# Delta rule: group decays from one product each, products ahead of the projections' barrier, blocks gathered before their ones

## The chip, the cores and the metric

The kernel runs on one core of one Trainium2 chip. Its engines work beside each other and meet at semaphores: PE (TensorE, matmuls into PSUM banks), DVE (VectorE), ACT (ScalarE), POOL (GpSimd) and SP, which issues the DMAs. The metric is the device time of one execution in microseconds (us).

## The reference

One layer of a hybrid network on 256 tokens of width 1024: modulation, input projections, a gated delta rule (8 heads, both directions), a state-space scan, an output projection and 32 experts of which 4 serve a token. What this change touches is the delta rule's triangular solve, per head and chunk of 64 tokens:

```python
G = jnp.cumsum(g, axis=-1)                        # g: log decay of a token
rel = G[..., :, None] - G[..., None, :]
kb = k * beta[..., None]
strict = idx[:, None] > idx[None, :]
lmat = jnp.einsum('bhncd,bhnsd->bhncs', kb, k) * jnp.exp(jnp.where(strict, rel, -jnp.inf))
mmat = lmat + jnp.eye(CHUNK, dtype=lmat.dtype)
rhs = jnp.concatenate([v * beta[..., None], kb * jnp.exp(G)[..., None]], axis=-1)
sol = lax.linalg.triangular_solve(mmat, rhs, left_side=True, lower=True, unit_diagonal=True)
```

Context and latent tokens make 512 tokens, 8 chunks of 64. The later scan over chunks uses `sol`; the experts come last.

## The kernel before

Every engine has its program written out by hand, in order. An engine marks a step on its own semaphore (`L.mark`) and another waits for that mark (`wait_ge(*L.at(engine, step, ...))`). All instructions of an engine run in the order in which the code issues them. The program has stages. In `proj` PE multiplies the tokens by the weight columns (`fm`, 20 of them) and by the modulation weights (`ada_chunk`, 12 of them), ACT copies and applies silu, DVE convolves (five taps a block, lines 1675 and 1680) and makes rows (`row_out`). At its end every engine marks `end` and waits for the other four (`barrier`).

The `delta` stage follows. Tokens lie in four tiles `t` of 128 (two chunks each); with two directions `d` this makes eight groups `G = 2t + d`, each of 8 heads x 64 columns = 512 columns. Tiles 0 and 1 are block `b = 0` of the solve, tiles 2 and 3 block 1. A group goes through these steps:

- POOL, `start_decay(G)` (line 2281), writes the mask less the second cumulative decay into one of four places, `DT[:, G % 4]`. From group 4 on it waits until group G - 4 is coupled.
- PE, `spread_decays(G)` (line 703), makes the first cumulative decay in a bank, by 16 products of 64x64: for each head and half a column of decays, broadcast, times a triangle of ones. An fp32 product is two matmul records in the trace, each with a weight load.
- DVE, `decay(G)` (line 1729), adds the two; ACT, `decays(G)` (line 1334), exponentiates; PE, `gram(t)` (lines 720, 725), makes k times k; DVE, `couple(G)` (lines 1740, 1743), multiplies into the matrix `MT`.
- POOL, `unit_diagonal(G)` (line 2307), puts ones on the diagonal by two selects.

Then, per block: PE gathers the 16x16 diagonal blocks (`gather_blocks`, line 735), DVE inverts them by substitution (`substitute`, lines 1751 to 1794, which leaves `Ysym`), PE scatters them back (`scatter_blocks`, line 746), DVE spreads them under masks into `X0` and `XT0` (`spread_inverses`, line 1807), and PE and DVE go up the levels 16 and 32 (`level_p`, line 760, `level` on DVE, `level_x`, `last_product`, `last_level`; lines 772 to 804), until `solved` (821, 833) forms W and U. Block 0 and 1 alternate on PE: gather 0, scatter 0, P 0, gather 1, the rest of level 0, scatter 1, and so on.

After this come the scan over the chunks (lines 849 to 983), the output projection (1022, 1028), routing, and the experts: a loop of turns, each of one expert and up to 64 rows (1097 to 1164). SP streams the expert weights in pieces of 2 MB through a ring of six.

## Time and profile before

| | |
|---|---|
| device time, three runs | 1454.61 us median, 1451.48 to 1460.07 |
| the profiled execution | 1451.1 us, span 1449.3 us |
| PE busy | 1276.2 us (88%) |
| DVE, ACT, POOL busy | 476.6, 253.0, 112.6 us |
| chain that ended last | PE 45%, DMA 28%, issue 4%, DVE 2%, ACT 2%, POOL 1% |
| mean DMA rate | 317 GB/s |

A share of busy time is a mean over the stages. The chain of waits is followed back from the last instruction: at each step to what released it. "issue" is time in which an engine waited for nothing that the profile shows. In a timeline row the bracket says how long the engine was idle before, and who ended it. The profiled execution is one run, so sums over its rows are to be held against its own 1451.1 us.

### The profile page before, as it was taken

Reading aid. Unit: us, or ns where it says so; the run is one execution under the profiler, and the core shown is the slowest. Engines: PE = TensorE matmul, PEld = TensorE weight load, DVE = VectorE, ACT = ScalarE, POOL = GpSimd, SP = SyncE. Lnnn points to the kernel's source line nnn. Section 1 sums busy time; section 2 is a strip of 40 time slices with the busy share of each in tenths; the row PEclk is TensorE's granted clock in tenths of the full one; section 3 lists DMA queues with packets and bytes.
Section 4 is the critical chain, followed back from the end, with each engine's and each line's share of the span. In section 5 each row is a group of like instructions: output and inputs, shape, how many; then the busy total and the mean of one; then the engine's idle time right before and its main releaser. Section 6 shows DMA issues by size and latency. Waiting matters only on the chain.

```text
span 1449.3 us, 27301 instructions
## 1 busy us (share of the span) xinstructions
PE 1276.2 (88%) x11256; PEld 593.7 (41%) x11257; DVE 476.6 (33%) x1023; ACT 253.0 (17%) x491; POOL 112.6 (8%) x158
## 2 busy tenths in 40 slices
PE   6999999456898999989898889887998999999995
PEld 2555445356665434333333333332433433433432
DVE  1246345651785523222221222121322322322323
ACT  2321522113614111111111111100100100100101
POOL 0201410443411000000000000000000000000000
PEclk9999999655997999999999999999999999999998
DMA  9516273000057699999999999999999699969993
GB/s 361 239 35 226 73 269 124 2 26 12 7 211 282 284 427 428 428 429 427 427 427 428 428 428 428 428 427 427 426 427 427 261 428 427 428 284 412 428 427 151
DMA packets 47824, 458.88 MB, mean 317 GB/s; under 512 B 4369, under 2 KB 4753, under 8 KB 22673
## 3 DMA queue, kind: packets, MB, share of 16 engines
q1 hardware_dynamic: 47762, 457.96, 76.2%
q8 instruction: 50, 0.82, 0.2%
q14 instruction: 12, 0.10, 0.0%
HBM read 456.31 MB, written 1.05 MB: 316 GB/s over the span
## 4 chain that ended last, share of the span: by engine, by line
PE 45%; DMA 28%; issue 4%; DVE 2%; ACT 2%; POOL 1%; DVEq 0%; ACTq 0%; POOLq 0%
DMA arena<-in_w_up 28%; PE bank L1135 21%; PE bank L1164 8%; PE bank L1106 3%; PE bank L1097 2%; PE bank L1028 2%; ACT arena L1517 1%; PE bank L1128 1%; PE bank L760 1%; PE bank L1159 1%; PE bank L1081 0%; PE bank L872 0%; PE bank L833 0%; PE bank L778 0%; POOL arena L2307 0%
## 5 line engine op out<-in xcount | busy, mean ns | idle before, releaser
L1135 PE MATMUL bank<-arena 128*64 128x512 f32 x2176 | 481.8, 595 | 34.6 <-DMA arena<-in_w_up 19.3
L1135 PEld LDWEIGHTS bank<-arena 128*64 128x64 f32 x2176 | 155.3, 136 | 342.1 <-issue 265.7
L1164 PE MATMUL bank<-arena 128*64 128x512 f32 x1088 | 239.4, 592 | 0.0
L2175 DVE TENSOR_SCALAR arena<-bank 128x512 f32<-128x512 f32 x34 | 23.6, 693 | 389.8 <-PE bank L1135 389.8
L1164 PEld LDWEIGHTS bank<-arena 128*64 128x64 f32 x1088 | 79.0, 136 | 137.6 <-issue 135.2
L634 PE MATMUL bank<-arena 128*128 128x512 f32 (+1 forms) x320 | 122.4, 539 | 0.4 <-DMA arena<-in_wfm 0.4
L2156 DVE TENSOR_TENSOR arena<-arena,bank 128x512 f32<-128x512 f32 x140 | 86.6, 682 | 6.0 <-PE bank L1106 6.0
L634 PEld LDWEIGHTS bank<-arena 128*128 128x128 f32 x320 | 60.5, 192 | 60.5 <-issue 54.1
L1097 PEld LDWEIGHTS bank<-arena 128*128 128x128 bf16 x1680 | 60.3, 118 | 27.0 <-DVE arena L2179 25.8
L1106 PE MATMUL bank<-arena 64*128 64x512 f32 x280 | 69.6, 614 | 0.9 <-ACT arena L1519 0.9
L1097 PE MATMUL bank<-arena 128*128 128x64 bf16 x1680 | 64.1, 199 | 1.1 <-DVE arena L2097 1.1
L1519 ACT ACTIVATE arena<-bank 128x512 f32<-128x512 f32 x34 | 20.4, 599 | 253.2 <-PE bank L1164 253.2
L2177 DVE TENSOR_SCALAR arena<-bank 128x512 f32<-128x512 f32 x34 | 23.6, 693 | 112.4 <-PE bank L1135 112.4
L2101 DVE TENSOR_SCALAR arena<-arena 96x64 bf16<-96x64 f32 x35 | 8.8, 251 | 156.8 <-PE bank L1164 156.8
L1511 ACT ACTIVATE arena<-arena 128x512 f32<-128x512 f32 x34 | 21.5, 632 | 212.9 <-DVE arena L2175 212.8
L1680 DVE SCALAR_TENSOR_TENSOR arena<-arena 128x512 f32<-128x512 f32 (+1 forms) x80 | 55.2, 690 | 2.8
L1511 ACT ACT_TABLE_LOAD x16 | 20.5, 1283 | 192.6 <-DVE arena L2175 192.6
L1513 ACT ACTIVATE arena<-bank 128x512 f32<-128x512 f32 x34 | 20.4, 600 | 190.2 <-PE bank L1097 190.2
L1106 PEld LDWEIGHTS bank<-arena 64*128 64x128 f32 x280 | 24.1, 185 | 45.8 <-issue 45.0
L1159 PE MATMUL bank<-arena 96*64 96x512 bf16 x68 | 13.8, 401 | 27.1 <-ACT arena L1517 27.1
L2164 DVE TENSOR_SCALAR arena<-arena 128x128 f32<-128x128 f32 x68 | 20.6, 346 | 43.0 <-issue 27.1
L567 PE MATMUL bank<-arena 128*128 128x512 f32 x64 | 29.7, 620 | 2.2 <-ACT arena L1207 2.2
(336 smaller groups left out, 1101.0 us busy)
## 6 DMA issues: line engine op xcount, KB each, us to landing
arena<-in_w_gate SPq DMA_DIRECT2D x64, 2048.0 KB, 21.2
arena<-in_w_up SPq DMA_DIRECT2D x64, 2048.0 KB, 22.8
arena<-in_w_down SPq DMA_DIRECT2D x64, 2048.0 KB, 20.7
arena<-in_w_ada SPq DMA_DIRECT2D x12, 2048.0 KB, 9.2
arena<-in_wfm SPq DMA_DIRECT2D x20, 512.0 KB, 6.5
arena<-in_wz SPq DMA_DIRECT2D x2, 2048.0 KB, 19.8
arena<-in_w_out SPq DMA_DIRECT2D x2, 2048.0 KB, 8.8
arena<-in_x SPq DMA_DIRECT2D x2, 1024.0 KB, 9.9
```

The lines of the kernel that those rows point to most:

```text
L567: last = mm(ps[t], xmT[:, k, base:base + 128], ada[:, m, k, :], start=(k == 0), stop=(k == KT - 1))
L634: last = mm(dst, win[:, i % 3, k, :], cols_, start=(k == 0), stop=(k == KT - 1))
L1028: last = mm(ps[2 + 2 * t + c_], mixT[:, k, 128 * t:128 * t + 128], wout[:, k, 512 * c_:512 * c_ + 512], start=(k == 0), stop=(k == KT - 1))
L1097: last = mm(ps[2][:, SLOT * k:SLOT * k + SLOT], hparts[:, s_, t, 512 * (k // 4) + k % 4:512 * (k // 4) + 512:4], Sb[:, t, :], start=(n == ...
L1106: last = mm(ps[3 + 2 * t + c_], GT[r, t, :], ysb[r, :], start=True, stop=True)
L1135: last = mm(ps[m][64 * c_:64 * c_ + 64, :], xcT[:, k, :], ring[:, 2 * h_ + m, k % 4, 512 * c_:512 * c_ + 512], start=False, stop=(k == KT ...
L1159: mm(ps[2][64 * c_:64 * c_ + 64, :], selb[0:96, :], bias[0:96, 2, 512 * c_:512 * c_ + 512], start=True, stop=False)
L1164: last = mm(ps[2][64 * c_:64 * c_ + 64, :], hidT[:, k % 4, 64 * (k // 4):64 * (k // 4) + 64], ring[:, 4 + h_, k % 4, 512 * c_:512 * c_ + 5 ...
L1511: f(hid[:, 1], hid[:, 0], ACT.Sigmoid, scale=ALPHA).then_inc(*L.mark("sig"))
L1680: v.scalar_tensor_tensor(out=dst, in0=src, scalar=convw[:, wi, tap:tap + 1], in1=dst, op0=ALU.mult, op1=ALU.add).then_inc(*L.mark("conv", i))
L2156: v.tensor_tensor(acc[:, t, s_], acc[:, t, s_], ps[3 + 2 * t + c_][:, :], ALU.add).then_inc(*L.mark(*(("acc",) if L.turn is not None else ...
L2175: v.tensor_scalar(hid[:, 0], ps[0][:, :], LIMIT, None, ALU.min).then_inc(*L.mark("a"))
```

## The change

1. `spread_decays(G)` on PE is one product of 128x512 instead of 16 of 64x64: the matrix `same` (ones within a chunk) times `steps[:, G]`. POOL makes `steps` in eight products ahead of its `end` mark, triangle times decay, as soon as `ada_chunk(10)` has been read (they lie in that chunk's memory).
2. PE marks its `end` but no longer waits at the barrier. It waits instead for the few steps whose banks or tiles it uses. The other four engines keep the barrier.
3. The groups have eight decay places (`DTs`): four more lie in the memory of `kdS`. `start_decay` of groups 4 to 7 waits for nothing but POOL's own steps. The products go to banks 0, 1, 4, 5, 0, 1, 0, 1.
4. `gather_blocks(b)` waits for the coupling (`MT`) instead of the ones. POOL writes the ones of block b after the gather and after `Ysym` b, and `level_p(b)` waits for them.
5. `kdS` is written after the last coupling. DVE spreads the inverses of block 0 ahead of the couplings of groups 6 and 7. ACT issues one exponential of a single column at the start of `delta`.

```diff
-            barrier(pe, L, "proj")
...
             def spread_decays(G):
 
-                t, d = divmod(G, 2)
-                if G >= 2:
-                    pe.wait_ge(*L.at("dve", "rel", G - 2))
-                for head in range(H):
-                    for half in range(2):
-                        r = slice(64 * half, 64 * half + 64)
-                        last = mm(ps[G % 2][r, 64 * head:64 * head + 64],
-                                  gA[r, t, d * 8 + head:d * 8 + head + 1].broadcast_to([64, 64]),
-                                  tri[r, d, 64 * half:64 * half + 64], start=True, stop=True)
-                last.then_inc(*L.mark("Gb", G))
+                pe.wait_ge(*L.at("pool", "steps", G))
+                if G >= 4:
+                    pe.wait_ge(*L.at("dve", "rel", (0, 1, 4, 5)[G - 4]))
+                mm(ps[g_bank[G]], const("same"), steps[:, G].rearrange("p h c -> p (h c)"), start=True, stop=True).then_inc(*L.mark("Gb", G))
...
             def gather_blocks(b):
 
-                pe.wait_ge(*L.at("pool", "unit", 4 * b + 3))
+                pe.wait_ge(*L.at("dve", "MT", 4 * b + 3))
...
             def level_p(b):
 
                 pe.wait_ge(*L.at("dve", "X0", b))
+                pe.wait_ge(*L.at("pool", "unit", 4 * b + 3))
...
+            pe.wait_ge(*L.at("act", "pad", NFM - 1))
+            pe.wait_ge(*L.at("act", "turned", TURNED[-1]))
             for G in range(4):
                 spread_decays(G)
+            pe.wait_ge(*L.at("pool", "kT", NKQ - 1))
+            pe.wait_ge(*L.at("act", "mod", 11))
             gram(0)
             gram(1)
+            pe.wait_ge(*L.at("dve", "row", 11))
             gram(2)
...
+            f(ssq[:, 0:1], const("eps"), ACT.Exp).then_inc(*L.mark())
             for G in range(8):
                 decays(G)
...
             decay(7)
+            spread_inverses(0)
             couple(6)
             couple(7)
-            spread_inverses(0)
...
             def start_decay(G):
 
                 t, d = divmod(G, 2)
-                if G >= 4:
-                    pool.wait_ge(*L.at("dve", "MT", G - 4))
                 pool.wait_ge(*L.own())
...
+            pool.wait_ge(*L.at("pe", "ada", 10))
+            for G in range(8):
+                t, d = divmod(G, 2)
+                pool.wait_ge(*L.own())
+                g_.tensor_tensor(steps[:, G], tric[:, d].unsqueeze(1).broadcast_to([P, H, C]),
+                                 gA[:, t, 8 * d:8 * d + 8].unsqueeze(2).broadcast_to([P, H, C]), ALU.mult).then_inc(*L.mark("steps", G))
...
             def unit_diagonal(G):
...
-                pool.wait_ge(*L.at("dve", "MT", G))
+                pool.wait_ge(*L.at("pe", "gathered", G // 4))
...
+            for G in range(4, 8):
+                start_decay(G)
             pool.wait_ge(*L.own())
             g_.memset(area("Y8"), 0.0).then_inc(*L.mark())
...
+            pool.wait_ge(*L.at("pe", "Gb", 7))
+            pool.wait_ge(*L.own())
+            g_.memset(area("XTf"), 0.0).then_inc(*L.mark("XTf"))
+            pool.wait_ge(*L.at("dve", "Ysym", 0))
             for G in range(4):
                 unit_diagonal(G)
-                start_decay(G + 4)
-            pool.wait_ge(*L.own())
-            g_.memset(area("XTf"), 0.0).then_inc(*L.mark("XTf"))
-            unit_diagonal(4)
-            unit_diagonal(5)
-            pool.wait_ge(*L.at("dve", "Ysym", 0))
-            unit_diagonal(6)
-            unit_diagonal(7)
             for G in range(4):
                 keg(G)
+            pool.wait_ge(*L.at("dve", "MT", 7))
             for t in range(2):
                 last_decays(t)
             pool.wait_ge(*L.at("dve", "Ysym", 1))
+            for G in range(4, 8):
+                unit_diagonal(G)
             for t in range(2, NT):
                 last_decays(t)
```

On POOL, from the start of `delta`, the rows stood like this before (L2319 the memset of `Y8`, L2307 the ones, L2281 `start_decay`, L2324 the memset of `XTf`):

```order
L2319 MEMSET arena 128x4x8
L2307 AFFINE_SELECT arena<-arena 128x512 x2
L2281 TENSOR_TENSOR arena<-arena 128x512
L2307 AFFINE_SELECT arena<-arena 128x512 x2
L2281 TENSOR_TENSOR arena<-arena 128x512
L2307 AFFINE_SELECT arena<-arena 128x512 x2
L2281 TENSOR_TENSOR arena<-arena 128x512
L2307 AFFINE_SELECT arena<-arena 128x512 x2
L2281 TENSOR_TENSOR arena<-arena 128x512
L2324 MEMSET arena 128x2048
L2307 AFFINE_SELECT arena<-arena 128x512 x8
```

Now they stand like this (L2285 `start_decay`, L2295 the steps, L2334 the memset of `XTf`, L2317 the ones, L2307 `keg`, L2323 `last_decays`):

```order
L2285 TENSOR_TENSOR arena<-arena 128x512 x4
L2295 TENSOR_TENSOR arena<-arena 128x512 x8
L2285 TENSOR_TENSOR arena<-arena 128x512 x4
L2329 MEMSET arena 128x256
L2331 MEMSET arena 128x4x8
L2334 MEMSET arena 128x2048
L2317 AFFINE_SELECT arena<-arena 128x512 x8
L2307 TENSOR_TENSOR arena<-arena 128x512 x4
L2323 TENSOR_TENSOR arena<-arena 128x512 x4
L2317 AFFINE_SELECT arena<-arena 128x512 x8
```

The ones have moved behind everything that the gather needs, and those of block 1 behind four `keg` and four `last_decays`.

On PE, from the end of the projections, it was before (L703 `spread_decays`, L720 `gram`; a number behind `x` is that of products):

```order
L678 MATMUL bank<-arena 128x512 [waits dve_proj,act_proj]
L703 MATMUL bank<-arena 64x64 [waits pe_proj,pool_proj,sp_proj,dve_proj,act_proj]
L703 MATMUL bank<-arena 64x64 x31
L703 MATMUL bank<-arena 64x64 [waits dve_delta]
L703 MATMUL bank<-arena 64x64 x15
L703 MATMUL bank<-arena 64x64 [waits dve_delta]
L703 MATMUL bank<-arena 64x64 x15
L720 MATMUL bank<-arena 64x64 x34
```

and at the gather (L735), two more groups behind it, the scatter (L746) and P (L760):

```order
L735 MATMUL bank<-arena 32x16 [waits pool_delta]
L735 MATMUL bank<-arena 32x16 x127
...
L746 MATMUL bank<-arena 32x32 [waits dve_delta]
L746 MATMUL bank<-arena 32x32 x63
L760 MATMUL bank<-arena 32x32 [waits dve_delta]
L760 MATMUL bank<-arena 32x32 x127
```

The same two places now (L703 again `spread_decays`, L717 `gram`; L732 gather, L743 scatter, L758 P):

```order
L682 MATMUL bank<-arena 128x512 [waits dve_proj,act_proj]
L703 MATMUL bank<-arena 128x512 [waits pe_proj,pool_proj,act_proj]
L703 MATMUL bank<-arena 128x512 [waits pool_proj] x3
L717 MATMUL bank<-arena 64x64 [waits act_proj,pool_proj]
...
L732 MATMUL bank<-arena 32x16 [waits dve_delta]
L732 MATMUL bank<-arena 32x16 x127
...
L743 MATMUL bank<-arena 32x32 [waits dve_delta]
L743 MATMUL bank<-arena 32x32 x63
L758 MATMUL bank<-arena 32x32 [waits dve_delta,pool_delta]
L758 MATMUL bank<-arena 32x32 x127
```

The first decay product no longer waits for SP or DVE, the gather waits for DVE instead of POOL, and P waits for POOL as well as DVE.

## Rows read from the trace of the kernel before

**Rows 1.** The page, part 2: granted clock of PE in 40 slices, in tenths.

```profile
PEclk9999999655997999999999999999999999999998
```

**Rows 2.** Chain of waits, 243 to 300 us: start, duration (us), what.

```profile
256.16 0.67 POOL arena L2307
256.96 0.67 POOL arena L2307
...
257.77 1.06 POOL arena L2281
...
291.11 2.55 PE bank L760 x170
```

**Rows 3.** Timeline, 230 to 292 us: start, busy us, instructions [idle before, releaser].

```profile
230.80 1.92 PE L518 MATMUL bank<-arena 128*32 128x512 f32 x16
...
243.01 1.02 PE L678 MATMUL bank<-arena 128*128 128x512 f32 x2
...
243.63 0.42 DVE L1675 TENSOR_SCALAR arena<-arena 128x256 f32<-128x256 f32 x1 [2.97 <-ACT arena L1293]
...
247.62 6.54 PE L703 MATMUL bank<-arena 64*64 64x64 f32 x125 [3.59 <-DVEq L1718]
...
249.83 0.69 DVE L1729 TENSOR_TENSOR arena<-bank,arena 128x512 f32<-128x512 f32 x1 [2.37 <-PE bank L703]
250.62 1.28 ACT L1334 ACT_TABLE_LOAD   x1 [4.04 <-DVE arena L1729]
...
251.92 1.15 ACT L1334 ACTIVATE arena<-arena 128x512 f32<-128x512 f32 x2
...
255.24 2.75 DVE L1743 TENSOR_TENSOR arena<-bank,arena 128x256 f32<-128x256 f32 x8 [0.27 <-PE bank L720]
...
266.29 2.69 PE L735 MATMUL bank<-arena 32*32 32x16 f32 x170 [8.27 <-POOL arena L2307]
...
270.06 1.46 PE L735 MATMUL bank<-arena 32*32 32x16 f32 x86 [1.08 <-issue]
...
271.56 0.69 DVE L1751 COPY arena<-bank 128x512 f32<-128x512 f32 x1 [6.42 <-PE bank L735]
...
285.43 1.28 DVE L1729 TENSOR_TENSOR arena<-bank,arena 128x512 f32<-128x512 f32 x2
...
285.57 2.04 PE L746 MATMUL bank<-arena 32*32 32x32 f32 x128 [9.71 <-DVE arena L1794]
...
289.76 2.49 DVE L1807 TENSOR_TENSOR arena<-bank,arena 128x512 f32<-128x512 f32 x4
```

**Rows 4.** Timeline at 329 us; queue row (packets, MB, share) of 291 to 372.

```profile
329.26 1.93 PE L760 MATMUL bank<-arena 32*32 32x32 f32 x128 [2.57 <-issue]
...
q8 instruction: 22, 0.36, 2.0%
```

**Rows 5.** Timeline: convolution taps beside POOL and alone; products on POOL.

```profile
160.09 4.49 DVE L1680 SCALAR_TENSOR_TENSOR arena<-arena 128x512 f32<-128x512 f32 x4
...
177.72 3.12 DVE L1680 SCALAR_TENSOR_TENSOR arena<-arena 128x512 f32<-128x512 f32 x4
...
356.09 4.40 POOL L2352 TENSOR_TENSOR arena<-arena 128x512 f32<-128x512 f32 x4 [11.40 <-PE bank L789]
```

**Rows 6.** Second block's steps; L833 in two stretches (busy, records, clock, DMA).

```profile
303.38 0.69 DVE L1751 COPY arena<-bank 128x512 f32<-128x512 f32 x1 [5.68 <-PE bank L735]
...
325.93 0.23 PE L760 MATMUL bank<-arena 32*32 32x32 f32 x1
...
334.00:345.00 11.00, 5.75 (x128) 5.63 (x128) 0.62 0.02 4
360.00:372.00 12.00, 4.31 (x128) 4.04 (x128) 0.88 0.02 4
```

**Rows 7.** Chain of waits at 597 us; instruction queue from 480 to the end.

```profile
597.44 25.69 DMA arena<-in_w_up
...
q8 instruction: 5, 0.08, 0.0%
```

More of the change, by code:

```diff
@@ L165, in lay_out_sbuf @@
     free = CONSTS["qmask"][0]
-    free = put(free, ("Z21", 128), ("T1", 128), ("own", 96), ("mX", 64), ("mQ", 64), ("negc", 128))
+    free = put(free, ("Z21", 128), ("T1", 128), ("own", 96), ("mX", 64), ("mQ", 64), ("negc", 128), ("tric", 128))
     assert free <= CONSTS["qmask"][0] + 256 * LEVELS.index(16)
@@ L299, in layer_program @@
         sM = DT
+        tric = view(area("tric"), 2, C)
+        steps = view(area("ada", 0, 4096), 8, H, C)
+        g_bank = (0, 1, 4, 5, 0, 1, 0, 1)
+        DTs = [DT[:, G] for G in range(4)] + [view(area("kdS", 512 * G, 512), H, C) for G in range(4)]
         xw = [view(area("MT", 2048, 2048), 2, 2, H, C), view(area("keG"), 2, 2, H, C)]
@@ L1333, in decays @@
                 act.wait_ge(*L.at("dve", "rel", G))
-                f(DT[:, G % 4], DT[:, G % 4], ACT.Exp).then_inc(*L.mark("DT", G))
+                f(DTs[G], DTs[G], ACT.Exp).then_inc(*L.mark("DT", G))
             def inverses(b):
@@ L1728, in decay @@
                 dve.wait_ge(*L.at("pool", "NG", G))
-                v.tensor_tensor(DT[:, G % 4], view(ps[G % 2][:, :], H, C), DT[:, G % 4], ALU.add).then_inc(*L.mark("rel", G))
+                v.tensor_tensor(DTs[G], view(ps[g_bank[G]][:, :], H, C), DTs[G], ALU.add).then_inc(*L.mark("rel", G))
             def couple(G):
@@ L1737, in couple @@
                 for par in range(2):
-                    bk, DT_ = ps[(6 if t == 2 else 2) + par], DT[:, G % 4, par:8:2]
+                    bk, DT_ = ps[(6 if t == 2 else 2) + par], DTs[G][:, par:8:2]
                     if t >= 2:
@@ L2234, in _ @@
                 g_.tensor_copy(negc[r], neg[r, :, 64 * half:64 * half + 64]).then_inc(*L.mark())
+                pool.wait_ge(*L.own())
+                g_.tensor_copy(tric[r], tri[r, :, 64 * half:64 * half + 64]).then_inc(*L.mark())
             own = view(area("own"), 3, 32)
@@ L2277, in start_decay @@
                 t, d = divmod(G, 2)
-                if G >= 4:
-                    pool.wait_ge(*L.at("dve", "MT", G - 4))
                 pool.wait_ge(*L.own())
-                g_.tensor_tensor(DT[:, G % 4], negc[:, d].unsqueeze(1).broadcast_to([P, H, C]),
+                g_.tensor_tensor(DTs[G], negc[:, d].unsqueeze(1).broadcast_to([P, H, C]),
                                  Gs[:, t, 8 * d:8 * d + 8].unsqueeze(2).broadcast_to([P, H, C]), ALU.subtract).then_inc(*L.mark("NG", G))
@@ L2319, in _ @@
             g_.memset(view(area("Y8"), 4, 64)[:, :, 0:64:9], 1.0).then_inc(*L.mark("Y8"))
+            pool.wait_ge(*L.at("pe", "Gb", 7))
+            pool.wait_ge(*L.own())
+            g_.memset(area("XTf"), 0.0).then_inc(*L.mark("XTf"))
+            pool.wait_ge(*L.at("dve", "Ysym", 0))
             for G in range(4):
                 unit_diagonal(G)
-                start_decay(G + 4)
-            pool.wait_ge(*L.own())
-            g_.memset(area("XTf"), 0.0).then_inc(*L.mark("XTf"))
-            unit_diagonal(4)
-            unit_diagonal(5)
-            pool.wait_ge(*L.at("dve", "Ysym", 0))
-            unit_diagonal(6)
-            unit_diagonal(7)
             for G in range(4):
                 keg(G)
+            pool.wait_ge(*L.at("dve", "MT", 7))
             for t in range(2):
```

## The prediction

> **What bounds the kernel now.** I read the page first, then the chain of waits, then the waits of PE, then the timeline around the places that the diff touches. Behind the projections, which end at about 247 us, the page's row of the granted clock falls to 0.6 and 0.5 for three slices [rows 1]: there PE often waits, and this is where the diff works. The chain of waits goes PE, DVE, POOL, DVE, PE there [rows 2, 3]. The reader is to see four things in it.
>
> First, the projections' barrier: PE's last projection product starts at 243.01, but the decay products start at 247.62, released by DVE, 3.6 us later [rows 3]. Second, POOL: after the first couplings (DVE, 255.24 to 258.0) POOL writes ones on the diagonal by pairs of selects 0.80 us apart, with a decay start of 1.06 us between pairs, and only when the fourth pair ends does PE gather the diagonal blocks, at 266.29 [rows 2, 3]. PE waited 8.3 us for it, and 9.7 for DVE's substitution behind it [rows 3]; no other wait of PE between 244 and 372 is as long. Third, that substitution runs from the copy at 271.56 to 285.51, and the level's product P starts at 291.11, after DVE has spread the inverses from 289.76 [rows 2, 3]. Fourth, from 291 on the PE waits for nothing but "issue": 128 matmul records run in 1.9 us, then 1.3 to 2.6 us of nothing. In the same stretch the instruction queue moved 22 blocks, 0.36 MB, so 16 KB each, one per 3.7 us [rows 4]. I read this as PE waiting for its instructions. A stretch so bound shifts with its start; it does not shrink by faster engines.
>
> The Trainium skill, "Runtime: NRT & Kernel Launch", Instruction fetch mechanics, also says that instructions come in blocks of 16 KiB, but calls the crossing of a boundary mostly hidden. By that sentence a product removed here would be worth nothing anywhere and the stretch would be set by the matmuls; the gap of 2.57 us in [rows 4] contradicts it.
>
> **The change part by part.**
>
> *One product per group instead of 16.* A group's decay took 32 matmul records (256 for eight groups), and takes 2 now: 240 records less, 1.9 blocks of 128. At 3.7 us a block that is 7.0 us if the PE were fetch-bound there, and 0 if it waits for others there. Six of the groups stand before the gather, two before the scatter, ahead of waits of 8.3 and 9.7 us [rows 3]; I take 0. The new product is 128x512 in fp32; the row product of that size took 1.02 us [rows 3]. Four of them from 244.1 end near 248, and grams 0 to 2, 128 records, near 250 (128 took 1.93) [rows 4], when DVE has done its adds.
>
> *Steps on POOL.* Eight products of 128x512 at 1.10 us (four took 4.40) are 8.8 us [rows 5]. They may start when the tenth ada chunk has been read, at 232.7 [rows 3], and end at 241.6. POOL was idle up to the barrier; PE wants the first at 244.1. They run beside DVE's convolutions. There the trace has a price: four convolution taps took 4.49 us beside POOL and 3.12 alone [rows 5]. Two such blocks are met in part: at most 2 times 1.4 us, against 2.97 us in which DVE idles before the last convolution [rows 3]. I take 0; were that idle time missing it would cost 2.8.
>
> The Trainium skill, "SBUF — State Buffer", Who interferes with whom, has a rule that speaks against this part: a DVE instruction with two SBUF inputs contends with a GpSimd instruction that reads SBUF. The 4.49 against 3.12 agree with it. By the rule each engine may block the other whole; even with the whole 2.8 us on POOL the last step would end near 244.4.
>
> *No barrier for PE.* DVE, ACT and POOL keep it, so the adds still start at 247.6. What goes is that PE's products stood behind it: the first add started at 249.83 [rows 3], now at 247.6, 2.2 us earlier. The exponential's table load of 1.28 us, which followed the first add [rows 3], now runs beside it.
>
> *From the barrier to the gather.* DVE: four adds at 0.64 (two in 1.28) are 2.6, eight couplings 2.75 [rows 3]: 247.6 + 2.6 + 2.75 = 253.0. ACT's first exponential can run at 247.6 + 1.28 + some 0.2 = 249.1, and four at 0.58 (two in 1.15) end at 251.4, so it is not late. The gather waits for the fourth coupling and no longer for POOL: 253.1 instead of 266.29, **13.2 us** earlier. Queued behind it on PE are the last two decays and gram 3, which DVE wants only after the substitution. The gather keeps its 5.2 us (266.29 to 271.5, one fetch gap of 1.08 within) [rows 3]. The four extra decay places let POOL start groups 4 to 7 at once (four at 1.06 from 247.6), so the fifth add no longer waits for POOL: two adds and the next couplings, 1.3 and 2.8 us, end at 257.1, before the gather does at 258.3. If they were late, the substitution behind them on DVE would be late by as much; with 1.2 us of room I take 0.
>
> *Substitution.* 13.95 us as before, from the copy at 271.56 to 285.51, where the scatter is released [rows 3]. Ysym is ready at 272.3 instead.
>
> *Ones behind the substitution.* POOL now writes them when Ysym is there, and the level's product P waits for the fourth pair: eight selects at 0.80 and two hand-overs of 0.1 are 6.6 us [rows 2]. Before, P started 5.6 us after Ysym (291.11 less 285.51) [rows 2]. So **1.0 us is lost** here. This is the new wait. It also hides the edit that puts the spreading before the last couplings: X0 would be ready 3.4 us after Ysym (scatter 2.04, half of 2.49, a hand-over) [rows 3], and nobody is waiting for it alone. Priced alone, that edit is worth between 0 and 2.2; I take 0.
>
> *The rest of the delta rule.* P starts at 278.9, and the fetch-bound chain follows, **12.2 us** earlier as a whole. The place of the block edges moves by 16 records or so, which is some 0.5 us either way and at worst one gap, 1.9. The second block's ones could be late too: its substitution starts with a copy at 303.38 [rows 6], so it ends at 317.3, now 305.1; the ones end at 311.7, and its P, at 325.93 before [rows 6], is due at 313.7. They are 2.0 us early. What POOL does behind them comes 6.5 us later against the chain; before 356.09 POOL idled 11.4 us [rows 5].
>
> *Experts.* No DMA is added or moved in SP's queue, and its waits are for steps of PE in this chain; the first expert pieces wait for PE's transposes of the mixed rows. So the weight stream moves with the chain, and with it the DMA waits that bound later turns, the first at 597.44 [rows 7]. The 12.2 us pass whole to the end.
>
> **The sum.** -13.2 + 1.0 = -12.2 on a profiled execution of 1451.1 us (span 1449.3, 1.8 around it): 1438.9. The three runs had a median of 1454.6, 3.5 above the profiled one; with that offset the forecast is 1442. What this kernel's measurement can tell from no change is about 0.5%, 7.3 us.
>
> **The rivals.**
>
> *A, the ones cost twice.* If selects beside DVE stretch as the taps did (1.44 times), eight take 9.2 instead of 6.4: 2.8 late at the first P and, less the 2.0 of room, 0.8 at the second; a block edge in a bad place adds 1.9. Gain 12.2 - 5.5 = 6.7, so 1448. For it: POOL gets both sets of ones at the moment when DVE goes on. Against it: the selects stood 0.80 apart in [rows 2] while DVE worked on banks, which is what it will do again behind both substitutions. Chance 0.13.
>
> *B, more than forecast.* In 334 to 345 PE is bound by its own products, at a mean clock of 0.62: one line's 128 records took 5.75 us there and 4.31 in 360 to 372 at 0.88 [rows 6]. If the moved stretch meets the full level (2.4 GHz) more often, this line and its neighbour give back up to 3.5: gain 15.7, 1439. It may as well go against, by as much; I count that in the range. Chance 0.10.
>
> *C, slower.* The experts' loop must stay in PE's instruction store: from 480 us to the end only 5 blocks came on the instruction queue [rows 7], in 34 turns of a loop. The change moves the loop against the 16 KB edges. If a turn then had to fetch once more, at a gap of about 1.9 us, 33 turns would cost 63: 1442 + 63 = 1505. It decides as soon as more than 10 turns pay. Against it: the loop is no longer than before, and touches three blocks of 16 KB in either program. Chance 0.05.
>
> *Forecast*: 0.72.
>
> **How the numbers follow.** The predicted time is the forecast's, 1442. Its own range, 1438 to 1447, is the block edge, the clock, and the 3 us by which medians of three runs differ (before: 1451.5 to 1460.1). A and B lie at its edges, so 1435 to 1450 leaves out C and the tails. Faster by over 0.5%: most of the forecast (0.66), all of B (0.10), a third of A (0.04), 0.80. Within: 0.15. Slower: C, 0.05.
>
> **What would show it.** Right: the gather on PE starts near 253 and is released by DVE; the level's first product is released by POOL's select, near 279; the add of group 0 starts at 247.6 with no wait for PE; the gaps from 280 on are still "issue", 22 blocks or so; turns of experts as before. Wrong: the gather waits for ACT or for POOL's steps; the second P is released by POOL; instruction blocks fetched in most expert turns; DVE's adds later than 248.

## The result, and the profile after

The changed kernel runs in 1446.41 us (median of 8 runs, 1442.0 to 1451.61), the kernel before beside it in 1454.86 (8 runs, 1451.48 to 1460.07). The ratio is 0.9934, with a 95% interval of 0.9913 to 0.9955: 9.6 us faster, between 6.5 and 12.7. The forecast was 1442, range 1435 to 1450. Its gain of 12.2 us, a ratio of 0.9916, lies inside the interval; its time is 4.4 us below the median. The profiled execution took 1448.96 us, 10 more than the sum of the prediction.

| | before | after |
|---|---|---|
| span of the profiled execution | 1449.3 us | 1447.1 us |
| PE busy | 1276.2 us | 1279.4 us |
| POOL busy | 112.6 us | 123.0 us |
| instructions; instruction blocks on q8 | 27301; 50 | 26834; 48 |

The timeline of the changed kernel where [rows 3] stood, PE, DVE, ACT and POOL mixed (start, busy us, instruction; in brackets idle before and releaser):

```profile
234.07 10.08 POOL L2295 TENSOR_TENSOR arena<-arena 128x512 f32<-128x512 f32 x8 [46.86 <-PE bank L522]
...
238.51 4.72 DVE L1684 SCALAR_TENSOR_TENSOR arena<-arena 128x256 f32<-128x256 f32 x4
...
244.24 1.02 PE L682 MATMUL bank<-arena 128*128 128x512 f32 x2
...
244.86 0.42 DVE L1679 TENSOR_SCALAR arena<-arena 128x256 f32<-128x256 f32 x1 [0.17 <-ACT arena L1296]
245.31 2.05 DVE L1684 SCALAR_TENSOR_TENSOR arena<-arena 128x256 f32<-128x256 f32 x4
...
245.57 3.68 PE L703 MATMUL bank<-arena 128*128 128x512 f32 x8 [0.30 <-PEq L688]
...
249.12 2.49 DVE L1733 TENSOR_TENSOR arena<-bank,arena 128x512 f32<-128x512 f32 x4 [0.42 <-DVEq L1722]
251.52 2.74 DVE L1747 TENSOR_TENSOR arena<-bank,arena 128x256 f32<-128x256 f32 x8
...
254.31 3.38 PE L732 MATMUL bank<-arena 32*32 32x16 f32 x221 [1.07 <-DVE arena L1747]
...
259.87 0.69 DVE L1755 COPY arena<-bank 128x512 f32<-128x512 f32 x1 [1.50 <-PE bank L732]
...
273.78 1.47 POOL L2317 TENSOR_SCALAR_AFFINE_SELECT arena<-arena 128x512 f32<-128x512 f32 x2 [8.37 <-DVE arena L1798]
275.45 1.47 POOL L2317 TENSOR_SCALAR_AFFINE_SELECT arena<-arena 128x512 f32<-128x512 f32 x2 [0.20 <-POOL arena L2317]
...
278.79 1.47 POOL L2317 TENSOR_SCALAR_AFFINE_SELECT arena<-arena 128x512 f32<-128x512 f32 x2 [0.20 <-POOL arena L2317]
...
280.36 2.25 PE L758 MATMUL bank<-arena 32*32 32x32 f32 x152 [4.65 <-DVE arena L1747]
284.27 1.61 PE L758 MATMUL bank<-arena 32*32 32x32 f32 x104 [1.67 <-issue]
```

The order of events is the one forecast: products behind the projections without a pause, adds, couplings, gather, ones behind the substitution, P. The wait of 4.65 us before P is put down to a coupling, but the couplings that P waits for (groups 0 to 5) had ended at 258.4; what ended at 280.26 is POOL's last select. Both programs are best compared from the last row product of the projections (L678 of before, L682 of after), because its own time changes from execution to execution; "at 36.1" below means 36.1 us behind that product. Against it the gather starts at 10.07 us instead of 23.28 and P at 36.12 instead of 48.10: 13.2 and 12.0 us earlier, as the sum had it.

Then the gain shrinks in this execution. The first KV product (L943) starts 121.53 us behind the row product, before 129.60: 8.1 us are left. The read-out behind the scan (L967) starts at 154.93 against 156.16: 1.2 left. The router's product (L1084) stands at 209.48 against 212.30: 2.8 left. So 3.9 of the 12.0 us went between P and KV, and 6.8 in the scan, before 1.6 came back. Where the scan's part went stands in the chain of waits of after (start, us, what):

```profile
390.06 1.06 PE bank L921 x32
391.12 2.00 PE bank L870 x4
393.12 1.06 PE bank L943 x32
394.18 2.00 PE bank L870 x4
```

In the kernel before the same four products took this:

```profile
388.88 1.09 PE bank L872 x4
```

And the windows of after (us, busy and count of PE, PEld, DVE, ACT, POOL, granted clock, DMA share, GB/s):

```profile
366.00:382.00 16.00, 12.38 (x377) 9.98 (x368) 10.41 (x24) 13.35 (x47) 8.93 (x9) 0.86 0.01 3
382.00:400.00 18.00, 18.00 (x216) 12.39 (x220) 8.80 (x19) 3.73 (x16) 10.09 (x10) 0.50 0.26 90
```

The scan ran at the lower of the two clock levels (1.2 GHz) here, and PE, which elsewhere waits in it, became its bound.

### The profile page after: what moved, and what is told of

Same layout as the page of the kernel before. It is cut to its first block, busy times and chain, and to the rows that moved or that the text cites. A ratio compares the mean times of both kernels' runs of the same rounds, so it can differ in the third digit from the quotient of the medians.

```text
span 1447.1 us, 26834 instructions
## 1 busy us (share of the span) xinstructions
PE 1279.4 (88%) x11016; PEld 586.6 (41%) x11017; DVE 479.3 (33%) x1023; ACT 253.1 (17%) x492; POOL 123.0 (8%) x168
## 4 chain that ended last, share of the span: by engine, by line
PE 41%; DMA 28%; DVE 2%; ACT 1%; issue 1%; DVEq 0%; ACTq 0%
DMA arena<-in_w_up 28%; PE bank L1138 21%; PE bank L1167 8%; PE bank L1109 3%; PE bank L1100 2%; PE bank L1031 2%; PE bank L870 1%; ACT arena L1521 1%; PE bank L1131 1%; PE bank L1162 1%; ACT arena L1519 0%; PE bank L974 0%; PE bank L986 0%; PE bank L996 0%; PE bank L1042 0%
## 5 line engine op out<-in xcount | busy, mean ns | idle before, releaser
L2181 DVE TENSOR_SCALAR arena<-bank 128x512 f32<-128x512 f32 x34 | 23.6, 693 | 112.6 <-PE bank L1138 112.6
L1684 DVE SCALAR_TENSOR_TENSOR arena<-arena 128x512 f32<-128x512 f32 (+1 forms) x80 | 58.7, 733 | 2.8
```

The source lines that it names most:

```text
L1684: v.scalar_tensor_tensor(out=dst, in0=src, scalar=convw[:, wi, tap:tap + 1], in1=dst, op0=ALU.mult, op1=ALU.add).then_inc(*L.mark("conv", i))
```

## The experiments

Theory 1: the change brings some 12 us, and what the trace lost behind P is drawn anew in each execution (the clock's level, the arrival of instruction blocks). Rival: a part of the loss is built in.

**The same kernel again.**

> The changed kernel once more, for a second trace. In its first trace the gather came 13.2 us earlier after PE's last row product (10.1 us after it instead of 23.3), but only 1.6 us were left at the first expert turn: 4 us went in the stretch where PE waits for instructions, 8 us in the scan over the chunks, where the granted clock was 0.5 and the two input products of a step took 2.07 us instead of 1.13. Theory 'level': the scan's clock differs from execution to execution; this trace may have it at 1.0, and then the last transposes of the mixed rows come about 8 us earlier than in the first trace; over the runs the ratio stays between 0.990 and 0.996. Rival 'built in': the moved stretch always meets the scan at 0.5; the second trace has 2.07 us again, and the scan takes 8 us more than before in every trace.

Measured: 1445.55 us, ratio 0.9932 [0.9906, 0.9959], span 1441.8. The scan of this execution:

```profile
366.00:382.00 16.00, 11.95 (x380) 9.75 (x380) 11.52 (x27) 12.69 (x45) 9.27 (x9) 1.00 0.01 3
382.00:400.00 18.00, 15.69 (x446) 12.58 (x444) 13.56 (x27) 4.39 (x19) 12.05 (x12) 1.00 0.43 142
```

Same program, full level (2.4 GHz), and its chain runs mostly through POOL and DVE where PE stood in the other. The read-out starts at 145.28 and the router's product at 201.71: 10.6 us before the old kernel's. From KV to the read-out it took 25.0 us, the first execution 33.4: the level cost 8.4. The fourteen profiles of this document agree: the stretch from KV to read-out took 25.0 us in the five whose granted clock over it was 1.00, 26.4 to 27.0 in the seven at 0.94, 27.6 in the one at 0.89, and 33.4 in this first one at 0.68. In the window before, where the clock of the first execution already fell to 0.86, PE was busy for 12.38 us of 16 in one and 11.95 in the other: why the clock fell in one and not in the other stays open. The two also differ by 1.25 us at KV.

**PE's barrier back.**

```diff
             pe.nop().then_inc(*L.mark("end", "proj"))
+            barrier(pe, L, "proj")
```

> The changed kernel with PE's barrier put back. My theory: the first product ends 0.9 us after 3.5 us of delay, so DVE's first add starts 0.9 to 1.0 us later after the barrier and the fourth ends 1.5 us later, since a product takes 0.86 us and an add 0.64; the gather starts 1 to 1.5 us later after PE's last row product (11.1 to 11.6 us instead of 10.1). Rival: the couplings wait for ACT's exponentials anyway, and the gather moves by under 0.5 us.

Measured: 1452.08 us, ratio 0.9969 [0.9951, 0.9988]. The gather starts at 13.94 us, 3.9 later than without the barrier and more than either expectation had (11.1 to 11.6, or under 0.5 later). The timeline of this kernel:

```profile
248.82 5.37 PE L704 MATMUL bank<-arena 128*128 128x512 f32 x8 [3.59 <-DVEq L1723]
...
250.43 0.69 DVE L1734 TENSOR_TENSOR arena<-bank,arena 128x512 f32<-128x512 f32 x1 [1.77 <-PE bank L704]
```

Its window from 249 to 256, which holds its eight decay records, and the window of the repeated changed kernel that holds the same eight, from 247:

```profile
249.00:256.00 7.00, 7.00 (x134) 3.70 (x135) 3.42 (x6) 3.81 (x6) 4.62 (x6) 0.76 0.00 0
```

```profile
247.00:254.00 7.00, 6.70 (x139) 3.93 (x139) 6.40 (x13) 3.68 (x7) 2.96 (x3) 1.00 0.02 5
```

The barrier costs twice: the adds start later by 1.3 us (6.2 behind the row product instead of 4.9), and behind the wait of 3.6 us the clock was granted at 0.76, so that eight records took 5.37 us instead of 3.68. The second and third add came 1.4 to 1.5 us behind the one before, and the fourth started 3.3 us later than without the barrier. The 1.7 us that the eight records took longer are what the clock added; by that estimate the barrier at full clock would cost the other 2.2. The lower clock is no accident of one execution: from 4.6 to 11.6 us behind the row product it was granted at 0.58 to 0.76 in all four profiles in which PE waits at the barrier (both of before, part 4 alone, this one), and at 1.00 in all ten in which it does not. The time is 6.5 us above that of the repeated changed kernel, timed beside it, where P is only 3.5 to 3.8 later; the difference is within the intervals and no run explains it.

**Sixteen products per group again**, over the broadcast decay as before; POOL's steps are still made and waited for.

```diff
-                mm(ps[g_bank[G]], const("same"), steps[:, G].rearrange("p h c -> p (h c)"), start=True, stop=True).then_inc(*L.mark("Gb", G))
+                t, d = divmod(G, 2)
+                for head in range(H):
+                    for half in range(2):
+                        r = slice(64 * half, 64 * half + 64)
+                        last = mm(ps[g_bank[G]][r, 64 * head:64 * head + 64],
+                                  gA[r, t, d * 8 + head:d * 8 + head + 1].broadcast_to([64, 64]),
+                                  tri[r, d, 64 * half:64 * half + 64], start=True, stop=True)
+                last.then_inc(*L.mark("Gb", G))
```

> The changed kernel, but a group's decay is again 16 products of 64x64; POOL still makes its steps, which nobody uses. The prediction priced the single product at 0, as work ahead of a wait: then the gather starts within 0.5 us of 10.1 us after the last row product, and P and the second gather too. Rival: the 240 more matmul records cost up to 1.9 instruction blocks of 3.7 us, 7 us, since the stretch before the gather is no longer covered by a wait for POOL; then the gather ends 2 to 4 us later.

Measured: 1447.33 us, ratio 0.9949 [0.9921, 0.9977]. The gather starts at 10.06, unchanged: the records ahead of it cost nothing, as the prediction took. Behind it they cost a little: DVE's copy starts at 16.22 instead of 15.62 and 15.34, and P at 36.70, 0.6 to 0.9 later, the router's product at 204.14. There are 50 instruction blocks instead of 48. That the two blocks cost time later is possible (1.8 us between the medians), but the intervals overlap: open.

**Before, with part 4 of the change alone**: the gather waits for the coupling, the ones stand behind the substitution, P waits for them.

```diff
-                pe.wait_ge(*L.at("pool", "unit", 4 * b + 3))
+                pe.wait_ge(*L.at("dve", "MT", 4 * b + 3))
...
                 pe.wait_ge(*L.at("dve", "X0", b))
+                pe.wait_ge(*L.at("pool", "unit", 4 * b + 3))
...
-                pool.wait_ge(*L.at("dve", "MT", G))
+                pool.wait_ge(*L.at("pe", "gathered", G // 4))
...
```

> The kernel before with one part of the change alone: the blocks are gathered after the coupling, ones are written behind the substitution, P waits for them; four decay places, 16 products, PE at the barrier. Theory: DVE's fourth coupling ended at 258.0, so the gather starts near 258.1 instead of 266.3 on the clock of the first trace, 8.2 us earlier after the last row product (15.1 us instead of 23.3), and P starts 7 us earlier. The other parts are then worth 5 us of the 12. Rival: the four decay places alone hold the couplings of groups 4 and 5, the substitution is late by several us and less than 5 us is left at P.

Measured: 1450.85 us, ratio 0.9967 [0.9946, 0.9988]. The gather stands at 14.55, 8.7 us earlier than before. About 8.3 of them are the wait for POOL's ones; the other 0.4 is that the fourth coupling itself ended 0.4 earlier, in an execution whose clock behind the barrier was 0.76 and not 0.58. P stands at 41.29, 6.8 earlier (expected: 7), and KV at 123.68. Of the 13.2 us at the gather the barrier is 3.9, and the remaining 0.6 (14.55 against the 13.94 of the kernel with the barrier) is the single product and the places.

**Ones beside the substitution.**

```diff
-            pool.wait_ge(*L.at("dve", "Ysym", 0))
             for G in range(4):
                 unit_diagonal(G)
```

> The changed kernel, but POOL writes the first block's ones as soon as the blocks are gathered, beside DVE's substitution, not behind it. In the changed kernel's two traces the level's first product P starts 36.1 and 35.8 us after the projections' last row product, 6.7 us after Ysym. Theory 1 (the ones behind the substitution are the 1.1 us that the change loses): POOL's selects run while DVE works through chains of small instructions whose time is mostly their fixed cost, the substitution keeps its 14.0 us, P waits for the spread alone and starts 3.4 to 4 us after Ysym, about 33 us after the row product, and the kernel is 2.5 to 3 us faster than the changed one (ratio to the kernel before 0.991). Rival (contention): selects and substitution stretch each other as taps and POOL did (4.49 against 3.12); the 6.6 us of selects lengthen the substitution by 2 us or more, P starts at 35 or later, and the kernel is within 1 us of the changed one.

Measured: 1443.24 us, ratio 0.9902 [0.9865, 0.9939]. P is at 34.96, 0.9 to 1.2 us earlier: both mechanisms happened. POOL and DVE in this kernel:

```profile
274.60 2.79 POOL L2317 TENSOR_SCALAR_AFFINE_SELECT arena<-arena 128x512 f32<-128x512 f32 x2 [0.20 <-POOL arena L2317]
```

```profile
270.22 2.85 DVE L1780 TENSOR_TENSOR arena<-arena 128x512 f32<-128x512 f32 x2
273.10 1.22 DVE L1783 TENSOR_REDUCE arena<-arena 128x128 f32<-128x1024 f32 x1
274.36 2.51 DVE L1786 TENSOR_TENSOR arena<-arena 128x512 f32<-128x512 f32 x2
...
279.29 1.21 DVE L1798 COPY arena<-arena 128x64 f32<-128x64 f32 x2
```

The same lines without selects beside them, in the changed kernel:

```profile
265.80 2.06 DVE L1780 TENSOR_TENSOR arena<-arena 128x512 f32<-128x512 f32 x2
267.89 1.22 DVE L1783 TENSOR_REDUCE arena<-arena 128x128 f32<-128x1024 f32 x1
269.14 2.05 DVE L1786 TENSOR_TENSOR arena<-arena 128x512 f32<-128x512 f32 x2
...
273.28 0.34 DVE L1798 COPY arena<-arena 128x64 f32<-128x64 f32 x2
```

A pair of selects grew from 1.47 to as much as 2.79 us, the two groups of products by 0.8 and 0.5. P stands 3.45 us behind the scatter instead of 6.7, but the scatter comes 2.1 to 2.3 later (21.4 us behind the gather instead of 19.1 to 19.4). Not all of this is the selects: `keg`, which follows them on POOL, started early too, at 279.27, and beside it the two copies that end the substitution (L1798) took 1.21 us instead of 0.34. The reduction, which reads one input, kept its 1.22. By the Trainium skill, "SBUF — State Buffer", Who interferes with whom, a DVE instruction with two SBUF inputs contends with a GpSimd one that reads, and a reduction never does; the rows of the products and of the reduction agree.

**Ones waited for piece by piece.** POOL writes the pairs in P's order.

```diff
-                pe.wait_ge(*L.at("pool", "unit", 4 * b + 3))
...
                     for u in range(16):
+                        if u % 8 == 0:
+                            pe.wait_ge(*L.at("pool", "unit", 4 * b + u // 4 + d))
...
-            for G in range(4):
+            for G in (0, 2, 1, 3):
                 unit_diagonal(G)
...
-            for G in range(4, 8):
+            for G in (4, 6, 5, 7):
                 unit_diagonal(G)
...
```

> The changed kernel, but P waits for the ones piece by piece: the first quarter of its products for the first pair of selects, and so on, and POOL writes the pairs in the order of P. Theory 1: P starts when the spread is there, 3.4 to 4 us after Ysym (about 33 us after the last row product instead of 36), and its last quarter no earlier than the fourth pair, 6.7 us after Ysym; it ends 1.5 to 2.5 us earlier than now, the instruction block that it needs is fetched meanwhile, and the kernel is 1.5 to 2.5 us faster than the changed one. Rival: behind P the PE waits for instructions, one block per 3.8 us, and the gap that P now runs over falls elsewhere; gain 0 to 0.5.

Measured: 1441.45 us, ratio 0.9891 [0.9847, 0.9935]; P at 32.76, 3.1 to 3.4 us earlier. The selects keep their 1.47 us, and P now waits for the spread:

```profile
277.14 2.25 PE L759 MATMUL bank<-arena 32*32 32x32 f32 x152 [1.41 <-DVE arena L1812]
280.71 1.61 PE L759 MATMUL bank<-arena 32*32 32x32 f32 x104 [1.32 <-issue]
```

At the second P (67.25 against 71.03 and 72.60) and at KV (116.27 against 120.28 and 121.53) it is still there, which speaks against the rival. But the kernel with two edits undone, below, with the same PE code as the changed one and P at 35.9 and 36.1, has KV at 117.57 and 119.97, so a lucky execution of the changed kernel comes within 1.3 us of this one; over the four such profiles the mean is 119.8, 3.6 later. At the router's product only 0.6 is left in this profile (201.15 against 201.71): its scan took 26.4 us and the better of the other two 25.0, and from read-out to router it took 58.4 against 56.4.

**One instruction block more**: 64 products of the second gather issued twice.

```diff
+                    if b and c_ < 16:
+                        for i in range(4):
+                            r = quarter(i)
+                            own = slice(32 * i + 16 * (c_ // 16), 32 * i + 16 * (c_ // 16) + 16)
+                            last = mm(ps[(4, 0)[b]][r, 16 * c_:16 * c_ + 16], MT[r, b, :, 32 * (i % 2) + c_], ident[r, own],
+                                      start=True, stop=True)
                 last.then_inc(*L.mark("gathered", b))
```

> The changed kernel with 64 more products (128 matmul records, one instruction block of 16 KB) in the second gather, which write the same values once more. Theory (PE is bound by its instructions from P to KV): from the gather on all is 3.7 to 4.0 us later against the last row product, though the 128 records themselves run in 1.9 us; KV starts at 124 to 125.5 instead of 120.3 and 121.5, and the instruction queue moves 49 blocks instead of 48. Rival (the gaps are waits for other engines' data, which the profile does not name): the records fill gaps, and KV is later by 0 to 1.9 us.

Measured in one execution: 49 blocks. The product behind that gather (XQ) stands at 52.44, against 48.21 and 49.55: 2.9 to 4.2 us later, more than the 1.9 us in which 128 records run. At KV only 0.9 is left against one profile of the changed kernel and nothing against the other (121.15; 120.28, 121.53). So the block costs its interval where it stands, but the spread of the arrivals behind it is as large. At KV the theory's 124 to 125.5 did not come, and what came (nothing to 0.9) is in the rival's range. That PE is bound by its instructions is supported at the one place, not shown for the stretch.

**Two edits undone**: places shared, and spreading behind the last couplings.

```diff
-        DTs = [DT[:, G] for G in range(4)] + [view(area("kdS", 512 * G, 512), H, C) for G in range(4)]
+        DTs = [DT[:, G % 4] for G in range(8)]
...
-            spread_inverses(0)
             couple(6)
             couple(7)
+            spread_inverses(0)
...
             for G in range(4, 8):
+                pool.wait_ge(*L.at("dve", "MT", G - 4))
                 start_decay(G)
...
```

> The changed kernel with two of its edits undone: groups 4 to 7 of the decays share the places of 0 to 3 again (POOL starts each behind its coupling), and the spreading stands behind the last couplings again. The prediction took both at 0. If that holds: gather at 10.1 us after the last row product as in the changed kernel, the substitution starts at 15.6 to 16.0, P at 35.8 to 36.2, released by POOL's ones. If the places matter, the adds of groups 4 and 5 wait for POOL and the substitution's copy starts later than 16.5; if the spreading matters, P is released by DVE, at 36.5 to 39, since decays 6 and 7 (1.3), couplings 6 and 7 (2.8) and the spread (3.4) add up to 7.5 us behind Ysym against the ones' 6.7.

Measured in one execution: gather at 10.07, the copy at 15.63, P at 36.11. POOL's last select ended at 36.0, so P was still released by the ones. At P both edits are worth nothing, as taken. But this execution needed 81.5 us from P to KV, and the changed kernel 84.4 and 85.4, which asked for another run:

> The kernel with the two edits undone (shared places, spreading behind the last couplings) once more, now timed. Its one profile had 81.5 us from the first P to the first KV, where the changed kernel had 84.4 and 85.4. Theory 1 (drawn anew in each execution): this profile has 82 to 85 us, and the ratio to the kernel before is that of the changed kernel, 0.993, within 0.002. Rival (the two edits cost what the trace of the changed kernel lost): 81 to 82 us again, and a ratio of 0.991 or less.

Measured: 84.1 us this time, and 1444.09 us, ratio 0.9927 [0.9902, 0.9952]. The same program drew 81.5 and 84.1. In both profiles the second P stands at 68.92 and 69.93, 1.1 to 3.7 us ahead of the changed kernel's, where DVE still has to couple groups 6 and 7 between the spreading and the first level; whether the edit costs something there, two profiles of each and the times do not tell.

**The kernel before once more.**

> The kernel before once more, for one profile. Theory 1 (how long PE takes from the first P to the first KV is drawn anew in each execution, since each of the 22 instruction blocks arrives after 3.4 to 4.0 us): the stretch takes 82 to 85 us, where the profile before had 81.5 and the profiles of the changed kernel 84.4 and 85.4; the last row product starts anywhere from 243 to 250, with the granted clock of the first 72 us. Rival (built in: the change put the block edges in worse places, and the stretch of the kernel before is short): again 81.0 to 82.0. In both, gather at 23.3 and P at 48.1 after the last row product, within 0.3.

Measured: 1454.54 us, gather at 23.17, P at 47.97, P to KV 82.6 us (81.5 in the first profile), router's product at 215.91 (212.30). The kernel before has now 81.5 and 82.6, kernels with the changed PE code 81.5 to 85.4 in four profiles, with means of 82.0 and 83.9. The two ranges overlap, but a built-in loss of some 2 us is not excluded. The first profile of before had drawn well at the start and from P to the router's product.

The start is the largest draw. The last row product, behind identical work, started at 243.01 in before and at 250.34 in the kernel with part 4 alone. Their first 36 us:

```profile
0.00:36.00 36.00, 23.57 (x115) 7.99 (x116) 5.33 (x21) 7.97 (x13) 0.20 (x4) 0.95 0.96 361
```

```profile
0.00:36.00 36.00, 20.98 (x87) 8.14 (x89) 5.32 (x21) 7.38 (x12) 0.20 (x4) 0.82 0.96 361
```

**Pieces, and x loaded later.**

```diff
-            sp.wait_ge(*L.at("pe", "scattered", 1))
+            sp.wait_ge(*L.at("pe", "W", 3))
             load("x", xin, x.rearrange("(t p) d -> p t d", p=P))
...
```

> The changed kernel with P waiting for its ones piece by piece, and with the load of x issued behind the last W product instead of behind the second scatter. In nine profiles the interval between instruction blocks that holds this load was 4.7 to 5.1 us, against a mean of 3.7 to 3.85. Theory 1 (load and instruction fetch share the DMA engines): no interval above 4.4 us remains between P and KV, the stretch is 1.0 to 1.5 us shorter than the 83.5 of the kernel with the pieces alone, and the ratio to the kernel before is 0.987 to 0.990. Rival: that interval is long for another reason (an instruction block that two engines want), and stays; ratio 0.989 to 0.992. Either way KV starts at 114.5 to 117 after the last row product (120.3 and 121.5 in the changed kernel).

Measured: 1441.28 us, ratio 0.99 [0.9869, 0.9932]. The x load was issued at 313.73 in the changed kernel; the gap of PE behind it:

```profile
320.72 1.93 PE L758 MATMUL bank<-arena 32*32 32x32 f32 x128 [3.34 <-issue]
```

In this kernel, at the same place (line 759), with the load at 359.47:

```profile
317.76 1.93 PE L759 MATMUL bank<-arena 32*32 32x32 f32 x128 [1.70 <-issue]
```

The long gap went: the block interval there is 3.5 us, where the twelve profiles with the load at its old place have 4.7 to 5.1. The interval that holds the later load is 5.3 us, but the kernel with the pieces alone has 5.5 there without a load. One of 4.6 us stands near 352 in this kernel with no load beside it, so "none above 4.4" was missed, and the load is not the only cause of a long interval. P to KV still took 83.4 us, and KV stands at 116.27 in both kernels: the load does slow a block, and moving it bought nothing that can be told.

**The second recurrence's decays as single products too**, over four steps that POOL writes into the place of x, whose load waits for them.

```diff
-                        last = mm(bk[r, 64 * head:64 * head + 64], gA[r, 2 + t, ch:ch + 1].broadcast_to([64, 64]),
-                                  tri[r, d, 64 * half:64 * half + 64], start=True, stop=True)
...
+                pe.wait_ge(*L.at("pool", "ssteps", G))
+                mm(bk, const("same"), ssteps[:, G].rearrange("p h c -> p (h c)"), start=True, stop=True).then_inc(*L.mark("sG", G))
...
```

> As the kernel before it in this list, and the four decays of the second recurrence (64 products, 128 matmul records) become one product each over steps that POOL makes, as the change did for the first eight; x is loaded once the fourth of them has been read. Theory 1 (PE is bound by its instruction blocks here, so 60 records fewer before KV are worth half a block, and 60 in the scan some of the other half): KV starts 1 to 2 us earlier than in the other kernel, the ratio to the kernel before is 0.985 to 0.988. Rival (POOL: 4.4 us more in front of its last keG groups, which W waits for): W2 is released by POOL and later by 1 to 2 us, ratio 0.989 or more.

Measured: KV at 113.74, 2.5 us earlier, router's product at 197.79 (199.09 with the pieces and x); yet 1445.88 us, ratio 0.992 [0.9893, 0.9948], outside the 0.985 to 0.988 of theory 1. The trace speaks for it, the timing does not: undecided. The best version on record is the one with the pieces, 1441.45 us, and with x moved 1441.28. Against the changed kernel's 1446.41 and 1445.55 that is some 4.5 us, of which the traces show 3 at P; the intervals still overlap.

## Why the prediction was right

*Barrier to gather.* The term was right in sum and nearly right in its parts. Forecast 10.1 us behind the row product (253.1 less 243.01), measured 10.07 and 10.06. Of the forecast 13.2 us, 8.2 are the wait for the ones and 5.0 the earlier fourth coupling (258.0 less 253.0): 2.2 for the first add and 2.8 for adds that follow each other without waiting for a product. Measured, the wait is about 8.3 and the earlier coupling 4.9, or 3.9 and 0.6 with 0.4 for the clock of that execution. What the prediction did not name is why the adds had been so far apart: behind the barrier PE's clock is granted at 0.58 to 0.76, and 1.7 of the 3.9 us are that. It came out right because the slow adds of the trace already held the low clock in them, and the new ones were priced by DVE alone.

*Steps on POOL.* 10.08 us instead of 8.8, so that they ended 0.1 us before the last row product and not 1.4; DVE's taps beside them took 4.72 us where four of the same shape alone take 2.05, 2.3 times as long and not the 1.44 times that the prediction had read off. The cover of 2.97 us in which DVE idled [rows 3] shrank to 0.17. It sufficed by 0.1 us on POOL and 0.17 on DVE, which is luck: the stretch was larger than the one priced, and the 2.8 us called the most that it could cost were used up. The first add started at 249.12, later than the 248 that was named as a sign of being wrong, but the row product was 1.2 later too: behind it the add stands at 4.9 us, forecast 4.6.

*Ones.* 1.0 us of loss forecast, 1.0 to 1.2 measured (13.2 at the gather, 12.0 and 12.3 at P); the selects took 1.67 us a pair, as worked out. The second block's ones ended 2.3 us ahead of its P, forecast 2.0. Nothing in the rows speaks for rival A.

*Single product, places, spreading at nothing.* The runs that undo them show it: nothing at the start of the gather, at P nothing for the places and the spreading and 0.6 to 0.9 us for the product, which the prediction had at 0.

*The rest shifts as a whole.* Half right. No new wait appeared behind P, and experts and their 5 instruction blocks stayed as they were, so rival C fell. From the router's product to the end it is 994.0 and 993.6 us in the two profiles of before and 993.4 and 994.0 in the two of the changed kernel, so what is gained at the router passes whole to the end, as the prediction said of the experts. But it took one execution's stretch for the kernel's. The stretch from P to KV took 81.5 to 85.4 us for one PE code, the scan lasted 25.0 to 27.6 us from KV to read-out in thirteen profiles and 33.4 in one, and the start differed by 7.3. Rival B asked only what the clock would give back, worth 3.5; the clock's real price was up to 8, in the other direction and in another place, in one of fourteen profiles, and 1.4 to 2.6 in eight of them. The offset of 3.5 us between profile and median of before, which the prediction carried over without a reason, is of this kind, and that adding it led nearer to the median (1442 and not 1438.9, measured 1446.4) is luck: its profile had the earliest row product of all fourteen and, of those with as many products in the stretch, the second shortest one.

*The size.* From row product to router's product the changed kernel took 209.5 and 201.7 us, the kernel before 212.3 and 215.9: 8.5 less on average; with the two profiles of the kernel with two edits undone (198.8 and 199.5), whose PE code is the same, it is 11.7. The timed difference is 9.6 (6.5 to 12.7), repeated 9.9, the forecast 12.2. The 2.3 to 2.6 us between forecast and measured gain lie within the interval, so they may be noise. If they are real, the fetch of instruction blocks behind P is the candidate (from P to KV 82.0 us on average before and 83.9 with the changed PE code); no run isolates it.

## What to carry to other kernels

Compare two traces from a common event behind the noisy start, not from zero, and take the same program's second profile before explaining a loss of a few microseconds. A barrier that PE does not need costs more than the delay of the first step behind it where the clock falls meanwhile: here 3.9 us for a first add that was 1.3 late. Where one engine hands over a tile in pieces, let the consumer wait for the pieces: it gave 3 us here, and running the producer beside the other engine gave one.

## What was not expected of the hardware

- The scan's 64x256 products took 2.00 us for four at a granted clock of 0.50 and 1.09 to 1.10 at 1.00, and the whole stretch from KV to read-out went with the clock (25.0 us at 1.00, 26.4 to 27.0 at 0.94, 33.4 at 0.68). Why one execution of a program gets the lower level there and another does not, the rows did not show.
- Behind PE's wait of 3.6 us at the barrier the granted clock was 0.58 to 0.76 in four profiles of four, and 1.00 at that place in all ten without the wait.
- The first 36 us were granted 0.82 to 0.95 in the same code, and the projections ended up to 7.3 us apart.
- Instruction blocks arrived 3.68 to 3.86 us apart on average over the stretch from P to KV (21 to 23 blocks in a profile), and the one behind the load of x after 4.7 to 5.1 us.
